# Moving the 32 rotary key columns of an input projection into the step sizes' weight tile

## The reference, cut to what matters

```python
h = _rmsnorm(x, lp['norm1_w']) * (1 + sc1) + sh1
u = h @ lp['w_in']
# state space heads
dt = softplus((u_ssd[..., D_SSD + CONV_DIM:].reshape(b, L, 2, H_SSD) + dt_bias))   # 16 columns
y_f, h_f = _directional_scan(ch, bh, xs * dt[:, :, 0, :, None], dt[:, :, 0] * a[0], h0[:, 0], False)
# latent attention heads
q_c = _rmsnorm(u[..., :Q_RANK], q_norm_w)
ckv = _rmsnorm(u[..., Q_RANK:Q_RANK + KV_RANK], kv_norm_w)                          # 128 columns
krope = u[..., Q_RANK + KV_RANK:]                                                   # 32 columns
```

## Time and profile before

| what | value |
|---|---|
| median of three executions | 1052.37 us (1051.87 to 1052.9) |
| span of the profiled execution, first to last instruction | 1048.6 us |
| TensorE matmul (PE) busy | 1026.5 us, 98% of the span, 6552 instructions |
| TensorE weight loads (PEld) busy | 938.2 us, 89% |
| VectorE (DVE) / ScalarE (ACT) / GpSimd (POOL) busy | 632.1 / 439.6 / 106.0 us |
| mean granted TensorE clock | 0.997 of full speed |
| moved by DMA | 159.56 MB, mean 152 GB/s |

### The profile page before, as it was taken

One profiled execution on the slowest core, in us unless ns is written; L12 is line 12 of the kernel. 1 busy time (PEld: TensorE's weight loads), 2 busy tenths in 40 slices (PEclk: granted clock), 3 DMA queues, 4 the chain that ended last, 5 costly groups with the idle time before them and its releaser, 6 DMA issues.

```text
span 1048.6 us, 16439 instructions
## 1 busy us (share of the span) xinstructions
PE 1026.5 (98%) x6552; PEld 938.2 (89%) x6552; DVE 632.1 (60%) x1134; ACT 439.6 (42%) x684; POOL 106.0 (10%) x99
## 2 busy tenths in 40 slices
PE   7899999999999999999999999999999999999995
PEld 4698995789999989999999999668999999999995
DVE  6686868868555543534448787886765555543333
ACT  3256445446333332343334655644543333233231
POOL 0004323003000000000100223400200000000100
PEclk9999999999999999999999999999999999999998
DMA  9843245214333478333364224451243333633331
GB/s 383 330 168 124 82 161 216 115 44 165 129 131 133 168 285 321 118 112 114 135 243 161 91 88 161 161 203 41 81 142 134 125 120 120 258 105 111 126 122 60
DMA packets 30678, 159.56 MB, mean 152 GB/s; under 512 B 3424, under 2 KB 4384, under 8 KB 19872
## 3 DMA queue, kind: packets, MB, share of 16 engines
q1 hardware_dynamic: 28896, 146.75, 38.4%
q10 hardware_dynamic: 1728, 12.06, 2.8%
HBM read 156.27 MB, written 2.52 MB: 151 GB/s over the span
## 4 chain that ended last, share of the span: by engine, by line
PE 93%; DVE 3%; ACT 1%; issue 1%; ACTq 1%; DVEq 0%
PE ps L475 26%; PE ps L477 26%; PE ps L476 26%; PE ps L504 3%; PE ps L920 2%; PE ps L900 1%; PE ps L719 1%; PE ps L746 1%; PE ps L909 1%; PE ps L571 1%; PE ps L823 1%; ACTq L1065 1%; PE ps L802 1%; PE ps L710 0%; DVE wlo L1353 0%
## 5 line engine op out<-in xcount | busy, mean ns | idle before, releaser
L475 PE MATMUL ps<-h_hi,whi 128*128 128x386 f32 (+1 forms) x1120 | 384.9, 344 | 0.2
L477 PE MATMUL ps<-h_hi,wlo 128*128 128x386 f32 (+1 forms) x1120 | 379.7, 339 | 0.0
L476 PE MATMUL ps<-h_lo,whi 128*128 128x386 f32 (+1 forms) x1120 | 378.7, 338 | 0.0
L1353 DVE TENSOR_TENSOR wlo<-stage,whi 128x2048 fp32r<-128x2048 f32 (+1 forms) x106 | 223.3, 2106 | 154.4 <-ACT whi L1015 154.4
L1015 ACT ACTIVATE whi<-stage 128x2048 fp32r<-128x2048 f32 (+1 forms) x106 | 185.9, 1754 | 229.1 <-PE ps L477 210.5
L475 PEld LDWEIGHTS ps<-h_hi,whi 128*128 128x128 f32 x1120 | 211.3, 189 | 9.7 <-issue 7.2
L476 PEld LDWEIGHTS ps<-h_lo,whi 128*128 128x128 f32 x1120 | 211.6, 189 | 0.3
L477 PEld LDWEIGHTS ps<-h_hi,wlo 128*128 128x128 f32 x1120 | 210.6, 188 | 0.0
L475 PE MATMUL ps<-hid_hi,whi 128*128 128x384 f32 x352 | 118.3, 336 | 0.0
L477 PE MATMUL ps<-hid_hi,wlo 128*128 128x384 f32 x352 | 118.3, 336 | 0.0
L476 PE MATMUL ps<-hid_lo,whi 128*128 128x384 f32 x352 | 118.3, 336 | 0.0
(11 more groups left out here) (295 smaller groups left out, 1146.4 us busy)
## 6 DMA issues: line engine op xcount, KB each, us to landing
stage<-wf_dram SPq DMA_DIRECT2D x44, 1024.0 KB, 4.8
adas<-wada_dram SPq DMA_DIRECT2D x80, 512.0 KB, 5.7
stage<-wf_dram SPq DMA_DIRECT2D x32, 704.0 KB, 4.1
stage<-win_dram SPq DMA_DIRECT2D x20, 1024.0 KB, 4.8
stage<-wout_dram SPq DMA_DIRECT2D x8, 1024.0 KB, 5.8
adaf<-wada_dram ACTq DMA_DIRECT2D x6, 1024.0 KB, 15.0
small<-small_dram SPq DMA_DIRECT2D x2, 1202.5 KB, 8.5
stage<-win_dram ACTq DMA_DIRECT2D x2, 1024.0 KB, 13.2
```

The lines of the kernel that those rows point to most:

```text
L475: mm(out, ah, bh, start=(k == 0), stop=False)
L476: mm(out, ah, bl, start=False, stop=False)
L477: return mm(out, al, bh, start=False, stop=(k == n - 1))
L1353: tt(wlo[:, g % 2, 0:width], stage[:, g % 2, 0:width], whi[:, g % 2, 0:width].bitcast(F32), ALU.subtract)\
```

## The change

The 32 rotary columns leave block 7 and join the step sizes' weights: the small tile grows from 16 to 48 columns for each contraction tile (`SIDE`), rotary columns first. Block 7 keeps the compressed keys alone: one output tile, 1024 weight columns, 24 matmuls. Its load, its two splits and its evacuation shrink with it. The step sizes now lie in rows 32 to 47 of their PSUM tile and of `nt`. ACT copies the 32 rotary rows to where they were before (`take_rotary_keys`, new semaphore `kr_in`): in layer 0 out of PSUM before it takes block 0, in layer 1 out of `nt` after it has split block 3. Readers of the rotary keys, and writers of the places that they are copied from, wait for `kr_in`. The permutation matmul takes 32 rows in place of 96. A smaller scratch region for descriptors makes room for the larger tiles.

```diff
+CKV_BLOCK, SIDE = 7, ROPE + 16
-        dthi, dtlo = sb("dthi", [P, P], F32R), sb("dtlo", [P, P], F32R)
+        dthi, dtlo = sb("dthi", [P, KD * SIDE], F32R), sb("dtlo", [P, KD * SIDE], F32R)
-        dt_stage = nt[:, 1, 0:P]
+        dt_stage = nt[:, 1, 0:KD * SIDE]
+        def win_width(n):
+            return KD * P if n == CKV_BLOCK else BLK
...
             def load_win(L, n):
-                load_w(L, n, win_d[L * N_WIN + n])
+                load_w(L, n, win_d[L * N_WIN + n][:, 0:win_width(n)], win_width(n))
...
-                for s in range(2):
+                for s in range(tiles):
                     for k in range(KD):
-                        last = split_mm(ps[:, b + s, 0:width], wtile(slot(L, n), 2 * k + s), hk(k, width), k, KD)
+                        last = split_mm(ps[:, b + s, 0:width], wtile(slot(L, n), tiles * k + s), hk(k, width), k, KD)
...
-                last = split_mm(ps[0:16, 6, 0:width], (dthi[:, k * 16:k * 16 + 16], dtlo[:, k * 16:k * 16 + 16]),
-                                hk(k, width), k, KD)
+                cols = slice(k * SIDE, (k + 1) * SIDE)
+                last = split_mm(ps[0:SIDE, 6, 0:width], (dthi[:, cols], dtlo[:, cols]), hk(k, width), k, KD)
...
-                wide_block(L, n, bank(n), width=TB if L else T, beside=beside)
+                wide_block(L, n, bank(n), width=TB if L else T, beside=beside, tiles=1 if n == CKV_BLOCK else 2)
...
                 pe.wait_ge(loga_ready, L * 2 + 2)
+                pe.wait_ge(kr_in, L + 1)
...
-                mm(ps[hrow, 7, 0:LAT], perm, u[hrow, U_KR, CTX:T], start=True, stop=True).then_inc(krot_ps, 1)
+                rrow = slice(KR0, KR0 + ROPE)
+                mm(ps[rrow, 7, 0:LAT], const[rrow, K_PERM + KR0:K_PERM + KR0 + ROPE], u[rrow, U_KR, CTX:T],
+                   start=True, stop=True).then_inc(krot_ps, 1)
...
                     if n < N_WIN - 1:
-                        split_hi(L, n + 2)
+                        split_hi(L, n + 2, win_width(n + 2))
+
+                def take_rotary_keys():
+
+                    if L:
+                        act.wait_ge(dt_taken, L + 1)
+                        src = nt[0:ROPE, 0, :]
+                    else:
+                        act.wait_ge(dt_used, 1)
+                        src = ps[0:ROPE, 6, 0:T]
+                    f(u[KR0:KR0 + ROPE, U_KR, :], src, ACT.Copy).then_inc(kr_in, 1)
...
+                if L == 0:
+                    take_rotary_keys()
                 act.wait_ge(small_in, L * 16 + 16)
                 if L == 0:
                     win_out(0)
...
                     first_taps(0)
                     split_next(1)
+                    take_rotary_keys()
                 f(expa[:], sc(C_ALOG, 16), ACT.Exp).then_inc(exps_ready, 1)
...
+                    elif n == CKV_BLOCK:
+                        last = tt(u[:, U_CKV, :], ps[:, b, 0:T], nv[:, 0, :], ALU.mult)
...
-                        split_lo(L, 6 + q)
+                        split_lo(L, 6 + q, win_width(6 + q))
...
                 pool.wait_ge(st_ps, L * 4 + 4)
+                pool.wait_ge(kr_in, L + 1)
...
-    wdt = blocks(w_in[:, :, 1280:1296], 16).reshape(n, P, P)
+    wdt = blocks(cat([w_in[:, :, 2704:2736], w_in[:, :, 1280:1296]], axis=2), SIDE).reshape(n, P, KD * SIDE)
```

More of the change, by code:

```diff
@@ L129, in program @@
         dt_split = sem("dt_split")
+        kr_in = sem("kr_in")
         dt_used = sem("dt_used")
@@ L436, in _ @@
                 sp.wait_ge(ck_ready, L * 3 + 3)
+                sp.wait_ge(kr_in, L + 1)
                 sp.dma_start(ckv_d[L], ck[:, 0:CTX]).then_inc(stored, 16)
@@ L590, in turn_dt @@
                 for c in range(NCH):
-                    last = tp(ps[:, 5, c * 16:c * 16 + 16], nt[0:16, 0, c * P:c * P + P], const[0:16, K_ID:K_ID + 16])
+                    last = tp(ps[:, 5, c * 16:c * 16 + 16], nt[ROPE:SIDE, 0, c * P:c * P + P],
+                              const[ROPE:SIDE, K_ID + ROPE:K_ID + SIDE])
                 last.then_inc(dt_tr, 1)
@@ L1102, in copy_out @@
                         last = f(upad[:, 2 * n:2 * n + 2, LATC + 2:LATC + 2 + LAT], ps[:, b:b + 2, CTX:T], ACT.Copy)
+                    elif n == CKV_BLOCK:
+                        last = f(u[:, U_CKV, :], ps[:, b, 0:T], ACT.Copy)
                     else:
@@ L1109, in add_shift @@
                     act.wait_ge(u_raw, n + 1)
-                    for a in range(2):
+                    for a in range(1 if n == CKV_BLOCK else 2):
                         for st, t0, t1 in streams:
@@ L1245, in _ @@
                 f(ck[:, P:2 * P], sc(C_CKV, P), ACT.Copy).then_inc(ck_ready, 1)
+                act.wait_ge(kr_in, L + 1)
                 f(kr[rrow, 0:CTX], u[rrow, U_KR, 0:CTX], ACT.Copy).then_inc(kr_ready, 1)
@@ L1501, in evac @@
                     b = bank(n)
-                    shifted_from(n % 2, b)
+                    shifted_from(n % 2, b, 1 if n == CKV_BLOCK else 2)
                     if n < 3:
@@ L1555, in _ @@
                 else:
-                    nc.vector.tensor_copy(shifted[0:16, 1, 0, :], ps[0:16, 6, T:TB])
-                    step(tt(nt[0:16, 0, :], ps[0:16, 6, 0:T], nv[0:16, 0, :], ALU.mult))
+                    side = slice(0, SIDE)
+                    nc.vector.tensor_copy(shifted[side, 1, 0, :], ps[side, 6, T:TB])
+                    step(tt(nt[side, 0, :], ps[side, 6, 0:T], nv[side, 0, :], ALU.mult))
                     for st, t0, t1 in streams:
-                        last = ts(nt[0:16, 0, t0:t1], nt[0:16, 0, t0:t1], shifted[0:16, 1, 0, st:st + 1], None, ALU.add)
+                        last = ts(nt[side, 0, t0:t1], nt[side, 0, t0:t1], shifted[side, 1, 0, st:st + 1], None, ALU.add)
                     last.then_inc(dt_taken, 1)
@@ L1726, in _ @@
                 tt(rt[rrow, 0, :], ps[rrow, 7, 0:LAT], sin, ALU.mult)
+                dve.wait_ge(kr_in, L + 1)
                 step(tt(kr[rrow, 256:512], u[rrow, U_KR, CTX:T], cos, ALU.mult))
@@ L2022 @@
     starts = (512, 768, 1024, 1296, 1552, 1808, 2320, None, 0, 256, 2064)
-    cols = [w_in[:, :, s:s + 256] if s is not None else
-            cat([w_in[:, :, 2576:2704], w_in[:, :, 2640:2736], np.zeros((n, D, 32), np.float32)], axis=2)
-            for s in starts]
-    win = blocks(cat(cols, axis=2), 256).reshape(n * N_WIN, P, BLK)
-    wdt = blocks(w_in[:, :, 1280:1296], 16).reshape(n, P, P)
+    wide = blocks(cat([w_in[:, :, s:s + 256] for s in starts if s is not None], axis=2), 256)
+    ckv = cat([blocks(w_in[:, :, 2576:2704], P), np.zeros((n, 1, P, BLK - KD * P), np.float32)], axis=3)
+    win = cat([wide[:, 0:CKV_BLOCK], ckv, wide[:, CKV_BLOCK:]], axis=1).reshape(n * N_WIN, P, BLK)
+    wdt = blocks(cat([w_in[:, :, 2704:2736], w_in[:, :, 1280:1296]], axis=2), SIDE).reshape(n, P, KD * SIDE)
     wout = arr(w_out).reshape(n, 2, KW2, P, 2, 4, P).transpose(0, 1, 4, 3, 5, 2, 6).reshape(n * N_WOUT, P, BLK)
```

11 lines of the change are left out of this document (6 added, 5 removed).

## The result

The kernel after took 1056.91 us (median of eight executions, 1055.2 to 1061.81); the kernel before, on the same chip, took 1052.4 us (eight executions, 1051.87 to 1055.32). The ratio is 1.0038, with a 95% interval of 1.0021 to 1.0055: slower, by more than the measurement is uncertain, and above the upper end of the forecast's range.

What follows compares the result with a forecast made beforehand. TensorE, busy 98% of the span, was taken as the bound, with DVE's chain next in round 2. 1048.6 - 0.54 + 1.25 or 2.5 + 3.8 outside the span gave 1053.7 us, range 1051.4 to 1055.4 us.

Steps and rivals of the forecast that it cites:

- Spacing of the matmuls: In block 7 one matmul costs 0.177 us, so removing 24 takes 4.25 us from TensorE's stream in each layer.
- The chain holds the values: In round 2 the values still wait for DVE's product; 0.54 us gained in all, the rest becomes TensorE waits.
- Added work at 0: The 48 columns, wider split, load grown from 64 to 192 KB, new copy and waits were taken to cost nothing.
- The price of the clock's fall: Behind round 2's two waits TensorE's clock may halve: 0 to 1.75 us per wait, 1.25 us taken where it falls.
- one fall or two: The clock falls behind one or both round 2 waits: 1053.1 or 1054.3 us, middle 1053.7 us; chance 0.55.
- The rival in which the clock comes back late: Behind round 2's waits the slow stretch lasts another 3.5 us, losing 1.75 us more per layer: 1057.8 us; chance 0.09.
- 3.8 us outside the span: Difference between the median 1052.37 us and the profiled span 1048.6 us, taken to stay after the change.
- The sum: Span 1048.6 us, less 0.54, plus 1.25 or 2.5 for falls, plus 3.8 outside the span: forecast 1053.7 us.

Runs made afterwards that it cites:

- e4: Changed kernel with DVE's round 2 reordered (evacuation and skip term before the scores, product before block 8's split): 1048.8 us, ratio 0.995 to the kernel before.
- e9: Kernel before the change with only DVE's round 2 reordered as in e4, block 7 keeping its 48 matmuls: 1052.02 us, ratio 0.9994.
- e5: Changed kernel with SP issuing layer 0's step sizes' load only after the first activations are in: 1057.05 us, one execution.
- e6: Changed kernel with the edits of e4 and e5 together: 1047.86 us, ratio 0.9964 to the kernel before.
- e1: Changed kernel with 24 idle matmuls, their result unread, put behind block 7: 1053.14 us, ratio 1.0001 to the kernel before.
- e3: Kernel before the change with block 7 cut to its first output tile and nothing added: 1058.63 us, ratio 1.0045.
- e2: Changed kernel with 12 idle matmuls, their result unread, put behind block 7: 1053.31 us, ratio 1.0006 to the kernel before.
- e7: Kernel before the change with four more idle products in TensorE's 1.7 us wait at the start: 1052.07 us, ratio 0.9997.
- e8: Kernel of e6 with the four more idle products of e7 at the start: 1047.51 us, ratio 0.9961 to the kernel before.

## Why the prediction was wrong

- **Spacing of the matmuls, 4.25 us a layer.** Right: (119.16 - 115.04) / 23 = 0.179 us.
- **The chain holds the values; 0.54 us gained, waits of 4.0 and 3.9 us.** Right in mechanism and in the waits (3.99 and 3.96). The gain was 0.14 + 0.23 = 0.37 us, because from the product's end to the values it took 123.49 - 123.34 = 0.15 us, where I took 0.06 from the start of the program. e4 and e9 show the chain as the cause: the same removal gains once the chain is shorter.
- **Added work at 0.** Right for the 48 columns, whose matmuls last 336 ns against 335, and for the split on ACT (507 ns against 294), which doesn't show in the time from ACT's first instruction to the step sizes' first matmul (16.12 us before and after). Wrong for the load: I had bounded 192 KB in place of 64 KB by 0 and 0.3 us, as time of the DMA engines. It was 0.5 us, by a way that I had not looked at: ACT's own issues take longer behind SP's longer load, and ACT starts later (e5, e6).
- **The price of the clock's fall: bounds 0 and 1.75 us a wait, 1.25 taken, one fall or two.** This is the step that failed. I took the first 3.5 us of the program's matmuls as the time that the clock needs to come back, and wrote that the slow stretch ends some 3.5 us from the fall or from the wait's end. It lasted 6.8 us in both layers, 6.1 and 6.2 us of it on work, and cost 2.74 and 2.82 us: 5.56 us in place of the 1.9 us in the middle of one fall and two. The factor I had used was if anything too high (0.45 us lost in each microsecond, not 0.5); the duration was wrong. I had also read one gap at the start, 1.6 us over which the clock held, as evidence that such a gap is harmless; in five of the eight other traces here that have this gap, 1.4 to 1.7 us long (e1, e3 to e6), the clock fell behind it. The rival in which the clock comes back late, 1057.8 us, had this mechanism with a loss of 3.0 us a layer, and is the one that happened; with 0.09 I had ranked it far too low. That its time lies within 0.9 us of the measured one is partly luck, since it has 2.0 us too much outside the span and lacks the 0.5 and 0.8 us below.
- **3.8 us outside the span.** Wrong as a reading: in the profiled executions here the time is 1.7 to 2.1 us above the span (1056.94 - 1055.2 = 1.74 after), and in no execution with a span on record more than 3.1 us. So the profiled execution before took, by estimate, some 1050.4 us and stood at the lower end of its kernel's scatter; its mean clock was 0.997, where the 58 other executions of the same kernel with a clock on record show 0.991 to 0.997 and spans of 1048.4 to 1054.3 us. I had set the profile of one execution against the median of others as if the difference were a constant. By luck this error ran against the others: without it the forecast would have been 1051.7 us, 5.2 us short.
- **The sum.** From 1053.7: + 3.7 (clock) + 0.5 (load) + 0.2 (smaller gain) + 0.8 (behind layer 0's loop) - 2.0 (outside the span) = 1056.9 us.

The Trainium skill, "TensorE: Matmul & The Clock Gate", section "HAM oscillation — how this bites in real kernels", had spoken against the change: a wait between bursts makes the next one start at the lower clock. The traces agree, with 0.50 behind waits of 3.99 and 3.96 us in after and in e3. Its section "The HAM clock gate" has it that what the chip looks at isn't tied to the program's start, by which like waits need not end alike. The traces agree: in e2 a wait of 1.91 us cost the clock and one of 1.85 us did not, and behind 1.57 us (e4) and 1.59 us (e6) in layer 1 it fell in one profiled execution and not in the other.

**Open.** The 0.8 us behind layer 0's loop: there TensorE's matmuls wait for transfers into `adas`, by another amount in each profiled execution (not at all in before, 0.2 us in after, where the weight loads wait 1.6 us more, 1.2 us in e1, and 1.0 us in e7 and 1.8 us in e3, which have no part of the change's additions), so I count it as scatter, without proof. And the clock's price in the other executions after: it isn't the same in each, since their mean clocks are 0.993 and 0.991 in the two fastest (1055.2 and 1055.42 us) and 0.988 and 0.986 in the two slowest (1059.4 and 1061.81 us), but only one execution has a trace, so where the clock fell in the others isn't known.

## What to carry to other kernels

Before taking work out of an engine that is 98% busy, look at what waits behind that work: if another engine's chain ends with it, the gain is nothing, and on TensorE the new idle time can cost more than the work did (8.5 us removed, 4.5 us lost). Shorten the covered chain in the same step, as e4, e6 and e8 do (1048.8, 1047.9 and 1047.5 us), and where the chain can't be shortened, keep the empty place filled, even with idle matmuls (e1), but not beyond the wait (e7). Price a fall of the clock by the stretch at the lower level that lies on work, times 0.45 here, and let the range reach 2.8 us for each wait.

## What was not expected of the hardware

The length of the stretch at 0.50 went with when it began. The table has every fall behind a wait of round 2 in a trace of this case, times from the windows' means as above. Falls that came while TensorE still waited lasted 6.8 us, falls that came after it had resumed 3.4 us.

| run, layer | wait, us | fall against the wait's end, us | at 0.50, us |
|---|---|---|---|
| after, 0 | 3.99 | - 0.8 | 6.8 |
| after, 1 | 3.96 | - 0.6 | 6.8 |
| e3, 0 | 3.99 | - 0.7 | 6.8 |
| e3, 1 | 3.96 | - 1.7 | 6.8 |
| e5, 1 | 3.96 | - 2.0 | 6.8 |
| e5, 0 | 3.99 | + 0.3 | 3.4 |
| e2, 0 | 1.91 | + 0.1 | 3.4 |
| e4, 1 | 1.57 | + 1.5 | 3.4 |
| e8, 1 | 1.58 | + 1.5 | 3.4 |

So the same wait of 3.99 us cost 2.74 us in after and 12.03 - 10.52 = 1.5 us in e5. The values of q = 2 and of q = 3 and the windows around the fall, in layer 0 of e5:

```profile
124.68 0.33 PE L757 MATMUL ps<-ew,xt 128*64 128x128 f32 x2 [3.99 <-DVE ew L1681]
...
136.71 0.33 PE L757 MATMUL ps<-ew,xt 128*64 128x128 f32 x2
```

```profile
124.00:125.00 1.00, 0.32 (x6) 0.35 (x8) 0.54 (x1) 0.00 (x0) 0.00 (x0) 0.99 0.32 57
...
128.00:129.00 1.00, 1.00 (x6) 1.00 (x6) 0.00 (x0) 0.84 (x2) 1.00 (x2) 0.80 0.01 0
```

At the start of the program this doesn't hold: TensorE had resumed each time, and the stretch lasted 10.2 us in e1, 6.8 us in e3 and 3.4 us in e4, e5 and e6. So what sets the length isn't shown.

In round 2 waits of 1.57 to 1.91 us were enough for a fall in some executions and not in others; 1.21 us (e4, e6, e8) never was in the traces here. At the start falls came behind waits of 1.38 us (e3), 1.54 us (e5) and 1.70 us (e1, e4, e6).

A load on SP that grew by 128 KB slowed the issuing of other loads on ACT, by 0.5 us in after.
